# The last product of a down piece issued as two, of 240 and of 272 columns

## The reference, cut to what matters

```python
D_MODEL, SEQ, DEPTH, D_FF = 1024, 256, 2, 2816

def swiglu(x, w_in, w_out):
    a, b = jnp.split(x @ w_in, 2, axis=-1)
    return (jax.nn.silu(a) * b) @ w_out

for l in range(DEPTH):                      # first block; the second has the same two networks
    x = x + 0.5 * swiglu(rmsnorm(x, ffn1_norm[l]), w_ffn1_in[l], w_ffn1_out[l])
    ...                                     # token mixing
    x = x + 0.5 * swiglu(rmsnorm(x, ffn2_norm[l]), w_ffn2_in[l], w_ffn2_out[l])
```

## Time and profile before

| what | value |
|---|---|
| median of three runs | 2608.09 us |
| profiled execution | 2608.56 us |
| its span | 2606.7 us |
| TensorE products, weight loads | 19726 of each |
| TensorE busy (products) | 2567.2 us, 98% of the span |
| weight loads busy | 2362.9 us, 91% |
| GpSimd busy | 2029.6 us, 78% |
| ScalarE busy | 1287.7 us, 49% |
| VectorE busy | 881.3 us, 34% |
| share of the last chain on TensorE | 92% |

### The profile page before, as it was taken

How to read it: one execution, slowest core, us unless ns; L and a number is a source line. 1 busy time by engine, 2 the same in 40 slices (tenths; PEclk the granted TensorE clock), 3 DMA queues, 4 the chain that set the end, 5 groups by cost and what they waited for, 6 DMA issues and landing times.

```text
span 2606.7 us, 48248 instructions
## 1 busy us (share of the span) xinstructions
PE 2567.2 (98%) x19726; PEld 2362.9 (91%) x19726; DVE 881.3 (34%) x1518; ACT 1287.7 (49%) x1934; POOL 2029.6 (78%) x906
## 2 busy tenths in 40 slices
PE   7999999999999999999999999999999999999998
PEld 6999999899899989989989998998998989898897
DVE  2744364211242436411121133733122131474212
ACT  4545555444444555544444455754444444574443
POOL 7988666898898866688888886478888878547886
PEclk9999999999999999999999999999999999999999
DMA  6566543555656654665555556245556556525554
GB/s 235 188 202 202 187 139 132 196 190 187 209 187 199 202 186 139 165 199 186 188 202 187 187 188 217 95 169 191 190 183 205 186 178 194 195 98 180 195 191 138
DMA packets 128738, 474.79 MB, mean 182 GB/s; under 512 B 14432, under 2 KB 14432, under 8 KB 127520
## 3 DMA queue, kind: packets, MB, share of 16 engines
q1 hardware_dynamic: 124704, 454.09, 52.6%
q0 software_dynamic: 3840, 17.83, 2.4%
HBM read 469.24 MB, written 2.62 MB: 181 GB/s over the span
## 4 chain that ended last, share of the span: by engine, by line
PE 92%; DVE 5%; ACT 2%; issue 1%; DMA 1%; POOL 1%; DVEq 0%; SPq 0%; ACTq 0%; POOLq 0%
PE psA L381 52%; PE psY L381 38%; PE psT L432 2%; DVE psY L1279 0%; POOL rest L1065 0%; DVE psY L1267 0%; PE psT L654 0%; ACT upper L1876 0%; DMA ring<-in_weights 0%; DMA cst<-in_consts 0%; DVE st L1364 0%; DVE x L1294 0%; ACT xT_upper L1876 0%; ACT G L1907 0%; DVE Sc L1339 0%
## 5 line engine op out<-in xcount | busy, mean ns | idle before, releaser
L1065 POOL TENSOR_TENSOR rest<-ring,upper 128x1024 fp32r<-128x1024 f32 (+1 forms) x834 | 1989.3, 2405 | 511.5 <-ACT upper L1876 500.5
L1876 ACT ACTIVATE upper<-ring 128x1024 fp32r<-128x1024 f32 (+1 forms) x834 | 869.9, 1053 | 774.4 <-DMA ring<-in_weights 773.8
L381 PE MATMUL psA<-xT_upper,upper 128*128 128x256 f32 x2784 | 384.6, 281 | 0.6 <-ACT arena L1876 0.6
L381 PE MATMUL psA<-xT_rest,upper 128*128 128x256 f32 x2784 | 383.1, 280 | 0.0
L381 PE MATMUL psA<-xT_upper,rest 128*128 128x256 f32 x2784 | 382.9, 280 | 0.0
L1320 DVE TENSOR_TENSOR psA<-sil,psA 128x256 f32<-128x256 f32 x144 | 61.8, 429 | 928.0 <-ACT sil L1876 927.9
L381 PEld LDWEIGHTS psA<-xT_upper,upper 128*128 128x128 f32 x2784 | 360.3, 189 | 12.7 <-ACT arena L1876 1.3
L381 PEld LDWEIGHTS psA<-xT_upper,rest 128*128 128x128 f32 x2784 | 351.7, 189 | 0.0
L381 PEld LDWEIGHTS psA<-xT_rest,upper 128*128 128x128 f32 x2784 | 351.2, 189 | 0.0
L381 PE MATMUL psY<-upper,hT_upper 128*128 128x512 f32 x704 | 200.1, 389 | 0.8 <-DVE hT_rest L1322 0.8
L381 PE MATMUL psY<-upper,hT_rest 128*128 128x512 f32 x704 | 200.0, 389 | 0.0
(11 more groups left out here) (282 smaller groups left out, 3003.6 us busy)
## 6 DMA issues: line engine op xcount, KB each, us to landing
ring<-in_weights SPq DMA_DIRECT2D x862, 512.0 KB, 3.5
G<-in_rows POOLq DMA_DIRECT2D x6, 1024.0 KB, 6.4
G<-in_rows POOLq DMA_DIRECT2D x7, 512.0 KB, 6.2
arena<-rel_by_distance POOLq DMA_DIRECT2D x8, 256.0 KB, 8.3
x<-in_x SPq DMA_DIRECT2D x2, 512.0 KB, 5.8
par<-in_params POOLq DMA_DIRECT2D x4, 256.0 KB, 5.8
xn<-in_mem POOLq DMA_DIRECT2D x1, 1024.0 KB, 11.8
memory_transposed<-arena POOLq DMA_DIRECT2D x1, 1024.0 KB, 5.5
```

The lines of the kernel that those rows point to most:

```text
L381: i = pe.matmul(out, lhsT, rhs, start=start, stop=stop)
L1065: pool.tensor_tensor(rest[:, r, 0:n], ring[:, r, 0:n], upper[:, r, 0:n], ALU.subtract)\
L1876: act.activation(out, in_, func, **kw).then_inc(*up)
```

## The change

`down` gets a flag that says whether an up piece is issued next. Where it is, the very last product of the down piece (third pass, second half of the tokens, second half of the columns) is issued as two products, of the first 240 and of the other 272 columns of the same 512. Both load the same hidden tile and write their part of the same bank. The flag is false for `down(0)` to `down(2)`. `tail` is not changed.

```diff
-                def down(j):
+                def down(j, up_next=True):
                     s = piece()
                     pe.wait_ge(*ready(j))
...
                     for w, v, first, last in passes():
                         for t in range(TT):
                             for n in range(2):
-                                mm(ys[2 * t + n], hT[v][:, j % HIDDEN, t * P:(t + 1) * P], s[w][:, n * 512:(n + 1) * 512],
-                                   first and j == 0, False)
+                                cut_at = S - 16 if up_next and last and (t, n) == (TT - 1, 1) else 512
+                                for c in (slice(0, cut_at), slice(cut_at, 512))[:1 + (cut_at < 512)]:
+                                    mm(ys[2 * t + n][:, c], hT[v][:, j % HIDDEN, t * P:(t + 1) * P],
+                                       s[w][:, n * 512 + c.start:n * 512 + c.stop], first and j == 0, False)
                     free()

                 up(GROUP, turn_group)
                 for j in range(GROUP):
-                    down(j)
+                    down(j, up_next=j == GROUP - 1)
```

## The result

The changed kernel takes 2615.16 us (median of 12 executions), the kernel before 2608.37 us on the same chip (12 executions): a ratio of 1.0028, with a 95% interval of 1.0019 to 1.0037. It is slower by 6.8 us, more than the 0.2% that can be told from nothing. The forecast was 2584.4 us, 24 us faster. The profiled execution took 2615.52 us, with a span of 2613.6 us for 2606.7.

A forecast was written before the change was run, and what follows sets the result against it. TensorE's pace was taken as the bound, waiting for nobody. 28.1 - 1.5 - 1.6 - 1.3 = 23.7 us off the profiled 2608.56 us gives 2584.9, forecast as a 2584.4 us median; own range 2579 to 2593, extended to 2610.

The forecast's parts named there:

- the two steps: 256-column products on TensorE: long step 117.7 ns in 134 of 136 up pieces, short step 113.3 ns, 4.4 ns apart.
- some nanoseconds at the hand-over pick the step: Entry from down to up piece: the split shifts alignment by up to 11.4 ns, giving the short step; chance 0.68.
- the term of 28.1 us: Up pieces: 133 pieces at the short step save 0.211 us each, 28.1 us in all.
- The pair: The split's two products: 117.7 + 120.4 = 238.1 ns for 226.7, 11.4 more; 1.5 us over 128.
- The way in and out: Both ends of an up piece: reaching the short step costs 0.013 us, leaving it 0.01; 1.6 and 1.3 us over 125.
- The supply: GpSimd, the next engine, goes from 87% to 90% busy at the short step; cost taken as 0.
- the long step holds: Up pieces: rival in which they keep the long step and only the split's cost is left, 2609.6 us; chance 0.19.
- restart: At each split: rival costing 0.09 us, 11.5 us over 128, with the long step behind, 2619.6 us; chance 0.07.
- The exceptions: Three up pieces with other products between them and the split: counted as they are, leaving 133 of 136 to gain.

The follow-up runs named there:

- The scans: Two runs of the changed kernel with a different cut at each site: 16-column steps, 2598.32 us; four-column steps from 196 to 316, 2594.86 us.

## Why the prediction was wrong, point by point

**What bounds the kernel, and the two steps: right.** TensorE's pace is the time, and the step of the up pieces is worth what was worked out: with 272 first, the kernel is 23.9 us faster (2608.25 less 2584.34; 20 to 27 by the interval of the ratio), where the forecast had 23.7. That the two agree to 0.2 us is luck; that they agree within the interval is not.

**The step that failed: "some nanoseconds at the hand-over pick the step", taken to mean that any shift by up to 11.4 ns will do.** I had three places where an entry by other products led to the short step and took the old alignment for the exception. At 240 columns the step did not change at any of the 125 sites: the term of 28.1 us measured 0, and an entry and an exit at the short step did not occur. The scans show both outcomes side by side, by cuts four columns apart: eight of 31 between 196 and 316 keep the long step. The reading of the earlier trace rows, that about 10 ns were enough, comes from starts rounded to 0.01 us; to the nanosecond the two last products in front take 461 and 458 ns, 3 ns apart. And the earlier trace rows had said it: two entries by the same code, one with the short step, one with the long. In the kernel after these two places have changed roles (starts 1521.22 and 2164.23 of the second row of eight):

```profile
1520.28 1.11 PE L381 MATMUL psA<-xT_upper,upper 128*128 128x256 f32 x8
1521.22 1.11 PE L381 MATMUL psA<-xT_rest,upper 128*128 128x256 f32 x8
...
2163.30 1.09 PE L381 MATMUL psA<-xT_upper,upper 128*128 128x256 f32 x8
2164.23 1.07 PE L381 MATMUL psA<-xT_rest,upper 128*128 128x256 f32 x8
```

A row that shows both outcomes of one code says that the outcome is a matter of place, and then an unknown shift is a draw: the chance of 0.68 for the short step was near what the scans make of it (20 of 31, 23 of 31), but one width on all sites is one draw for all of them, and this one lost. Only a trace of the new width could tell.

**The pair: right in sum, wrong in its parts.** Forecast 117.7 + 120.4 = 238.1 ns, measured 106.65 + 129.1 = 235.75; so 9.1 ns more in place of 11.4, or 1.2 us. I had the 240 columns held by their weight load. By the starts they are not: 106.6 ns is near their columns at the clean rate (106.3). The 272 behind them pay, 129 for 120.4.
The Trainium skill says that the spacing is set by the weight load and the product together and, for the isolated gap, N/2.4 + 2.5 ns ("TensorE: Matmul & The Clock Gate", Back-to-back issue gap). By that, as an estimate from the page's formula, the pair would take 218.3 ns, 2.5 more than an undivided 512; the trace has 235.8 and 9.1 more, and the measurement decides. That section's sustained figure for 512 columns, about 131 ns, does not fit either: 226.7 here.

**The way in and out: right where there is a short step.** With 272 first, the way in costs 12.5 ns (5452 or 5453 for 48 x 113.3, 5440) against 13, the way out 15 (231 233 231 for three 226.7) against 10.

**The supply: right at near 0.** With 272 first, GpSimd is busy 115.4 of the same 128.3 us, 90% as worked out from the earlier trace rows, and the longest wait of a `psA` product for its rests is 1.0 us, once. Products into `psY` waited 1.9 us in all for VectorE's `hT_rest`, in two places of the first network, where before it was 0.8 us in one.

**The rival "the long step holds" was the one that came, and it was priced too low.** Its rows of 1.10 came, by another mechanism: the alignment is not the old one after the pair, and the scans show that the way in is of account. I gave it 1.5 us and 2609.6, since I took down pieces as always even at 226.7 ns. They are even only because nothing had moved them. With the offset of this pair the up piece hands it on through 48 steps and nine products of the next down piece pay 44 ns. That is 5.6 us over 128, and with the pair's 1.2 the whole 6.8. The rival "restart" had the sign and a size that fits (from 0.041 us a split it decides, 0.053 were measured), but by another mechanism: the pair itself takes only 9 ns more.

**The exceptions.** `up(15)` behind the transpositions, short before (1.07 in the earlier trace rows), has the long step now (rows at 145.98 and 149.74 read 1.10 and 1.11). One such place is 0.2 us.

**What stays open.** Why a given offset ends in the one step or the other. The length of the pair does not order the outcomes: 3.3 ns more at 268 columns and 6.8 at 244 and 248 keep the long step, 5.6 to 6.6 at 252 to 264 and 272, and 12.3 at 236, give the short one. No record of the trace shows what holds the long step up by 4.4 ns a product.

## What to carry to other kernels

Where TensorE is the bound and one shape shows two paces in one trace, the entry may decide, and a split product in front is a way to shift it; but try several widths in one execution, one at each site, before one width goes on all of them. When a price is put on "nothing happens", follow the shift on to the next stage: a stream that has been even everywhere may be so only because it was always entered alike. And where two entries by the same code had different outcomes, an unknown shift has the chance of a draw, and all sites draw together.

## What the runs showed of the hardware that was not expected

- The step of an up piece is decided to four columns of one product in front of it (1.8 ns at the clean rate), and repeats: in two scans of 31 cuts the three or four sites of each cut with an up piece straight behind always agreed.
- At the cut of 240 the disturbance goes through 48 products at the long step unchanged: the nine uneven steps behind them (233 234 236 224 231 235 229 232 231 ns) are, to 1 ns, those straight behind the pair in the run that splits the first product (232 234 235 225 230 236 229 232 231). Over both scans, where an up piece follows the pair straight and a down piece comes next, that down piece paid nothing, 23 or 45 ns behind the long step, to 1 ns, and 14 to 16 behind the short one (but for one that began behind a wait of TensorE).
- By the recorded starts a short product is not held up itself, but the one behind it: 64 columns took 28 ns, and the 448 behind them 286, where the undivided 512 take 226.7.
- Counting from the starts to the nanosecond, the times are whole numbers of about 6.67 ns: a short step is 17 of them (113.3), 512 columns 34 (226.7), three long steps 53 (353.3), the 53 ns of a cycle 8. That is arithmetic on the starts, no mechanism that was tested.
